# Dense pieces between all six rounds of an inversion level, on one core

## What is computed

```python
def first_block(x, mem, ...):
    p = rmsnorm(x, norm_mix) @ w_in
    y_ret  = retention_mixer(p[..., :RET_PROJ], ...)        # 8 heads of 64
    y_rwkv = rwkv7_mixer(p[..., RET_PROJ:], ...)            # 8 heads of 64
    x = x + concat([y_ret, y_rwkv]) @ w_out
    x = x + memory_cross_attention(rmsnorm(x), rmsnorm(mem), w_q, w_kv, w_o)   # k, v = mem_n @ w_kv
    ...

def wkv7_scan(r, w, k, v, a, b):            # per head, state 64 x 64, over 512 steps
    sa = state @ a_t
    state = state * w_t + sa * b_t + v_t * k_t
    y_t = state @ r_t
```

## Time and profile before

| | us |
|---|---|
| median of three executions | 1638.69 |
| the three | 1635.54, 1638.69, 1638.96 |
| the profiled execution | 1636.71 |
| its span, first to last instruction | 1634.9 |
| PE busy in it | 1589.2 |
| mean granted clock of PE | 0.996 of full speed |

### The profile page before, as it was taken

How to read it: one execution, slowest core, us unless ns; L and a number is a source line. 1 busy time by engine, 2 the same in 40 slices (tenths; PEclk the granted TensorE clock), 3 DMA queues, 4 the chain that set the end, 5 groups by cost and what they waited for, 6 DMA issues and landing times.

```text
span 1634.9 us, 27099 instructions
## 1 busy us (share of the span) xinstructions
PE 1589.2 (97%) x11727; PEld 1287.0 (79%) x11727; DVE 887.9 (54%) x1386; ACT 669.2 (41%) x1005; POOL 121.0 (7%) x138
## 2 busy tenths in 40 slices
PE   7999999999999999999999999999999999999998
PEld 5856778786895898888888888777668888888887
DVE  5555586442634364555454664536975666554644
ACT  4316843325334264334141254656883432221210
POOL 1300106000000010000000020012300000000000
PEclk9999999999999999999999999999999999999999
DMA  7611232321630345536453533321003233233322
GB/s 245 182 52 52 77 90 100 104 84 44 196 132 23 129 129 185 180 107 227 129 180 130 180 84 112 78 78 53 4 25 103 74 107 94 88 103 103 99 76 84
DMA packets 154073, 176.66 MB, mean 108 GB/s; under 512 B 14600, under 2 KB 111506, under 8 KB 153570
## 3 DMA queue, kind: packets, MB, share of 16 engines
q1 hardware_dynamic: 145004, 162.24, 31.2%
q10 hardware_dynamic: 8950, 12.69, 2.6%
HBM read 168.31 MB, written 8.43 MB: 108 GB/s over the span
## 4 chain that ended last, share of the span: by engine, by line
PE 87%; ACT 5%; DVE 5%; DMA 1%; issue 1%; ACTq 0%; SPq 0%; POOL 0%; DVEq 0%
PE ps L397 64%; PE ps L848 4%; PE ps L1471 4%; PE ps L2908 1%; PE ps L2920 1%; DMA sb_arena<-sb_arena 1%; PE ps L3164 1%; PE ps L2940 1%; PE ps L2066 1%; DVE weights_low L420 1%; ACT weights_high L417 1%; PE ps L1049 1%; PE ps L765 1%; PE ps L824 1%; PE ps L1061 1%
## 5 line engine op out<-in xcount | busy, mean ns | idle before, releaser
L420 DVE TENSOR_TENSOR weights_low<-sb_weights_raw,weights_high 128x2048 fp32r<-128x2048 f32 (+2 forms) x117 | 263.8, 2255 | 259.4 <-ACT weights_high L417 259.3
L397 PE MATMUL ps<-left_high,weights_high 128*128 128x512 f32 (+1 forms) x888 | 352.0, 396 | 2.3 <-DVE left_low L718 2.1
L397 PE MATMUL ps<-left_high,weights_low 128*128 128x512 f32 (+1 forms) x888 | 345.9, 390 | 0.0
L397 PE MATMUL ps<-left_low,weights_high 128*128 128x512 f32 (+1 forms) x888 | 345.9, 389 | 0.0
L417 ACT CAST weights_high<-sb_weights_raw 128x2048 fp32r<-128x2048 f32 (+2 forms) x117 | 219.4, 1875 | 298.2 <-PE ps L397 261.7
L397 PEld LDWEIGHTS ps<-left_high,weights_high 128*128 128x128 f32 (+1 forms) x888 | 166.0, 187 | 47.5 <-issue 8.1
L397 PEld LDWEIGHTS ps<-left_high,weights_low 128*128 128x128 f32 (+1 forms) x888 | 166.0, 187 | 36.1
L397 PEld LDWEIGHTS ps<-left_low,weights_high 128*128 128x128 f32 (+1 forms) x888 | 166.1, 187 | 35.5 <-issue 1.7
L397 PE MATMUL ps<-weights_high,hidden_high 128*128 128x512 f32 x432 | 169.1, 391 | 0.0
L397 PE MATMUL ps<-weights_high,hidden_low 128*128 128x512 f32 x432 | 168.2, 389 | 0.0
L397 PE MATMUL ps<-weights_low,hidden_high 128*128 128x512 f32 x432 | 168.1, 389 | 0.0
(11 more groups left out here) (456 smaller groups left out, 2465.9 us busy)
## 6 DMA issues: line engine op xcount, KB each, us to landing
sb_weights_raw<-in_w_in SPq DMA_DIRECT2D x25, 1024.0 KB, 5.3
sb_yT<-in_ada_w SPq DMA_DIRECT2D x24, 1024.0 KB, 5.2
sb_weights_raw<-in_ffn_w_up SPq DMA_DIRECT2D x44, 512.0 KB, 4.7
sb_weights_raw<-in_mlp_w_up SPq DMA_DIRECT2D x16, 1024.0 KB, 5.7
sb_weights_raw<-in_mlp_w_down SPq DMA_DIRECT2D x16, 1024.0 KB, 7.5
sb_weights_raw<-in_ffn_w_down SPq DMA_DIRECT2D x10, 1024.0 KB, 5.1
sb_weights_raw<-in_xattn_w_kv SPq DMA_DIRECT2D x8, 1024.0 KB, 5.2
sb_weights_raw<-in_w_out SPq DMA_DIRECT2D x6, 1024.0 KB, 5.1
```

Source lines behind the costliest of these rows:

```text
L397: last = nc.tensor.matmul(o, lhsT, rhs, start=b["first"] and i == 0, stop=b["last"] and i == len(pairs) - 1)
L420: nc.vector.tensor_tensor(l[:, 0:n], raw[:, 0:n], h[:, 0:n].bitcast(F32), ALU.subtract).then_inc(w_low, 1)
```

## The change

Nothing is computed differently. The same pieces are dealt out to other places of the four lists.

- Front, PE only: 14 pieces instead of 13 stand ahead of retention, and none after its step 0. Four instead of three stand ahead of `lora_pe(pe, 0)`, and six instead of seven before `kk_pe`.
- Inversion, PE: four pieces instead of two between the grams and level 1. In levels 1 to 4 there are 3 after y01, 1 after r1, 1 after r2, 2 after r3, 1 after r4, and after r5 1 (levels 1 and 2) or 2 (levels 3 and 4). In level 5 there are 3, 2 and 5 instead of 5 and 5. The number up to the end of the stage is 56 as before.
- ACT and DVE: their steps move likewise. ACT takes 3 steps after the first two copies of a level, 1 between the third and the fourth, 5 after. DVE takes 5, 2, 1 and 1 around its adds.

```diff
@@ front1_pe
-            fill(dense, 13)
+            fill(dense, 14)
             for s in range(18):
                 retention_pe(pe, s)
-                if s % 2 or s < 4:
+                if s and (s % 2 or s < 4):
                     fill(dense, 1)
...
             memory_turn_pe(pe, range(4))
-            fill(dense, 3)
+            fill(dense, 4)
             pe.wait_ge(norm_low, pe.count(norm_low))
             lora_pe(pe, 0)
...
-            fill(dense, 7)
+            fill(dense, 6)
             kk_pe(pe)
@@ invert_pe
             gram_to_mask(3)
-            fill(dense, 2)
+            fill(dense, 4)
...
             for lv in LEVELS:
                 for last in side_by_side(y_of(lv, 0), y_of(lv, 1)):
                     last.then_inc(inv_y, 1)
-                fill(dense, 5)
+                fill(dense, 3)
...
                     xm_end, y_end = side_by_side(xm_of(lv, 0), y_of(lv, 2))
...
+                    fill(dense, 1)
                     xt_end, y_end = side_by_side(xt_of(lv, 0), y_of(lv, 3))
...
+                    fill(dense, 1)
                     for u in range(1, NPAIR):
                         xm_end, xt_end = side_by_side(xm_of(lv, u), xt_of(lv, u))
...
-                        if u == 1:
-                            fill(dense, 5)
+                        fill(dense, (2, 1, 2 if lv > 2 else 1)[u - 1])
                 else:
                     xt_end, y_end = side_by_side(xt_of(lv, 1), y_of(lv, 2))
...
+                    fill(dense, 2)
                     chunk_products(*y_of(lv, 3)).then_inc(inv_y, 1)
                     fill(dense, 5)
@@ invert_dve
                 add(lv, 1)
-                fill(dense, 5)
+                fill(dense, 2)
                 add(lv, 2)
+                fill(dense, 1)
                 add(lv, 3)
-            fill(dense, 5)
+                fill(dense, 1)
+            fill(dense, 3)
             add(5, 1)
-            fill(dense, 5)
+            fill(dense, 7)
```

## The result

The changed kernel takes 1644.17 us (median of six executions, 1642.71 to 1648.57) against 1635.84 us for the kernel before (six, 1634.56 to 1638.96). The ratio is 1.0048, with an interval of 1.0036 to 1.0061: 7.9 us slower, between 5.9 and 10.0. The forecast was 1642.4, slower by 3.75; the direction and the range held, and the forecast slowdown was half of what came. The profiled execution took 1644.51, with a span of 1642.7, 7.8 more than the span of before.

The account below looks back on a forecast made before the run. PE bounds the kernel, busy 97% of the span. Terms -0.6 - 0.55 + 5.1 - 6.5 + 1.8 + 2.8 + 0.4 + 1.2 + 0.1 = +3.75 on 1638.69 gave 1642.4 us, range 1634.5 to 1647.0.

Parts of the forecast that it names:

- Breaks: PE, levels 1 to 5: 17 more breaks of dense work by small runs, 0.30 us each, +5.1 (4.3 to 7.3).
- Gaps removed: PE's waits for instructions in the levels: 6.5 us lost before, removed, with 1.8 (0.6 to 3.0) left.
- no stop over 0.7 us inside small runs: Sign expected in the profile after, in PE's small runs, with such stops totalling 1.8 us.
- r4 of level 1: PE's round r4 waits for DVE's adds, which stand behind the weights step: +2.8 us, between 2.4 and 3.2.
- r4 of level 2: Same wait for the weights step, between the copies of y 2 and y 3: 6.24 against 5.87, +0.4 us.
- Piece 49: Level 5: PE reaches this piece before the weights step that makes its weights is done, +1.2 us.
- Ahead of level 1: Two more pieces cover PE's 0.54 us stand for DVE's add before the first round: -0.55 us.
- Front: Retention -1.35 us; LoRA products 0.78 later, carried on by ACT's chain as +0.77; net -0.6 (-1.35 to 0).
- (1): Rival, no change: the weights step doesn't hold PE and the three waits mostly fall away, -0.65, 1638.0 us; chance 0.27.
- (2): Rival, faster: a break costs nearly nothing and instruction gaps close entirely, -2.3 or more, down to 1634.2 us; chance 0.20.
- (3): Rival, slower: gaps are not fetches, or one falls into each level; +8.4, 1647.1 us; chance 0.11.
- (4): Rival: the change doesn't do what it says; excluded by the order, where rounds and pieces alternate.

Follow-up runs that it names:

- e7: Kernel before with e6's edits and, in levels 1 to 4, pieces as 4 behind y01, 3 behind r2, 3 behind r4: 1638.00 us against 1637.69.
- e10: Changed kernel with ACT's high part of the weights ahead of the copy of y 2 in level 1 alone: 1640.41 us against 1637.67 before.
- e6: Kernel before with the piece ahead of retention, four pieces instead of two ahead of level 1, five and three in level 5: 1638.62 us against 1637.69.
- e12: Changed kernel with weights step early, LoRA part of before, three ACT steps ahead of level 5's copy of y 2: 1634.95 us against 1637.67 before.
- e9: Changed kernel unedited, measured once more in another group: 1645.35 us against 1637.67 for the kernel before, ratio 1.0055.
- e4: Changed kernel with ACT's high part ahead of the copy of y 2 in levels 1 and 2, in level 4 for level 5: 1639.37 us against 1638.18 before.
- e8: Kernel before with the last gram product issued twice, so later PE instructions stand 32 matmul records further on: ratio 1.0003 to before.

## Why the prediction was right or wrong

- **Direction and range** held: slower, 1644.2 within 1634.5 to 1647.0. The size did not: +3.75 forecast, +7.9 measured. That the absolute number, 1642.4, lies only 1.8 from 1644.2 is luck: its base, the median of three executions, 1638.69, is 2.85 above the median of six, 1635.84, and that made up for most of what was missing. In the profile, the terms of the change come to +5.0 of the 7.8; the other 2.8 are the first products and the scan, below.
- **Breaks**, 0.30 each: right, 0.29 by the rows of after; 17 x 0.29 = 4.9, for the +5.1 of the sum.
- **Gaps removed**, 6.5, with 1.8 left: right in sum. After has 1.18 and 0.21 from start to start where a pitch is 0.03, and some 0.2 beside dense pieces, about 1.6. But the sign "no stop over 0.7 us inside small runs" failed: there is one of 0.96. The gaps are fetches, as the prediction took them to be. What it didn't have is that they stand at fixed counts; e7 shows that this matters, since its shorter runs didn't keep PE from standing 3.24 us at one of them.
- **r4 of level 1**, +2.8: the mechanism as forecast, link by link, and 3.16 in size (4.79 from the start of the two dense pieces ahead of r4 to r4, against 1.63 where PE doesn't stand), within the 2.4 to 3.2. What failed is that the step stopped there. Behind the stop half the clock follows in three profiles of four, 1.4 to 2.6 more, which is a term that the sum left at nothing. With the front's 1.35 it is up to 4.0, about the size of what is missing between 3.75 and 7.9; e10, 6.2 for one step of ACT, fits it. For the executions without a profile only the mean clock is known, so its share of the median isn't shown.
- **r4 of level 2**, +0.4: 1.35 measured (2.98 against 1.63). The step that failed is the low part's duration: 2.29 was taken, and it took 3.06, though POOL worked beside it for 0.9 us only. Who is first seems to matter: in the levels of the 14 profiles the 30 low parts that began while POOL was at work took 2.65 to 3.31, and the 50 others 2.28 to 2.30, also where POOL began behind them. PE's own path of 5.87 was 0.1 too long.
- **Piece 49**, +1.2: 1.27 measured (1.16 ahead of it and 0.10 at its slower first pitch), released by line 420 as forecast.
- **Ahead of level 1**, -0.55: right, the stop is gone. A second one in the grams, for DVE's add, fell from 1.43 to 0.43 in after and e6 and not in e12, so it is no term of the change.
- **Front**, -0.6: retention -1.6 for -1.35, LoRA +0.85 for +0.77. That the LoRA delay is carried on was right, but the step stopped short. The fourth piece is one that PE lacks later: it stands 2.78 for the same low part, where it had stood almost nothing. That alone loses no more than the 0.85, since the low part comes 0.14 later in the profile. But half the clock behind it cost 1.35 to 1.4 in three profiles of five. Net +0.6 with it, -0.75 without.
- **Scan** +1.9 and the first products +0.9 were in no term. In the other profiles the scan has 0 to +2.4 and down to -1.1, and the first products -0.3 to +1.2, with kernels that share the code: scatter between executions, not shown to come from the change. So one profile's place by place sum isn't the median's: e9, the same kernel, has +0.06 in the scan and +6.05 in the levels for +1.9 and +4.2, and ends at nearly the same +7.85.
- **Rivals.** (1), the waits gone, is what e4 made: +1.3 (-0.8 to +3.3) against the -0.65 of the text. In the changed kernel they came. (2) did not come: no break cost under 0.1. (3) did not come: 1.6 of the 6.5 are left in after, and e8 shows that the gaps go with the place in the instruction stream. (4) was excluded.

Taken together for the levels of the first profile: two pieces fewer behind level 1's start -1.4, breaks +4.9, stops -6.5 + 1.6, the three waits 3.2 + 1.35 + 1.3, the end +0.1: +4.55, against 4.2 measured.

## What to carry to other kernels

When dense work is cut finer to cover stops, look first at what else the pieces' list carries: here a weights step, shared with the copies on ACT, slid behind a result that PE had yet to produce. The stops that the finer cut closed (4.9 us) were spent on its breaks (4.9), and the waits came on top. A stop of about 3 us on PE should be priced with half the clock behind it, 1.35 to 2.6 us more, in a share of the executions, here in seven of ten cases. And a sum made from one profile misses terms that come in some executions only; a second profile of the same kernel shows them for little.

## What the runs showed that I had not expected

- Half the clock (1.2 GHz, the lower of the two levels; means of 0.50 to 0.68 in the windows shown) behind stops of PE of 2.8 to 3.2 us, in seven of ten such stops seen in the front and the levels, and behind none of 37 stops of 1.4 to 2.2 us: dense matmuls of 512 columns 0.43 for 0.23, a round 1.92 for 1.09. The same stop in the same kernel may be followed by it or not.
- Stops for instructions always at a count of 192 or 193 modulo 256 (40 of 40), with semaphore instructions counted, of 0.36 to 3.46 us, the same count costing 0.40 in e7, 1.29 in e6 and 2.34 in e8; and the end always 1.20 to 1.61 us behind the end of an instruction transfer.
- A low part that begins while POOL is at work takes 2.65 to 3.31 in place of 2.29 in the levels; one that POOL joins later keeps its 2.29.
